# Every third tile of peer_u multiplied whole in fp32 in the first expert pass

## The reference, cut to what matters

```python
    best, pos = lax.top_k(cand, PEER_TOPK)
    eidx = jnp.take_along_axis(cidx, pos, axis=-1)
    gate = jax.nn.softmax(best, axis=-1).astype(h.dtype)
    ...
    def expert_block(args):
        hx, ex, gx = args
        act = jax.nn.gelu(jnp.einsum('td,tkd->tk', hx, u_tab[ex]))
        return jnp.einsum('tk,tkd->td', act * gx, v_tab[ex])
```

## Time and profile before

| | |
|---|---|
| time, median of 3 runs | 3781.97 us (3767.97 to 3790.55) |
| span of the profiled execution | 3785.3 us |
| first expert pass in it | from about 765 to 1495 us |
| second expert pass in it | from 1495 to about 2105 us |
| busy over the span | PE 90%, DVE 70%, PEld 71%, ACT 34%, POOL 12% |

### The profile page before, as it was taken

How to read it: one execution, slowest core, us unless ns; L and a number is a source line. 1 busy time by engine, 2 the same in 40 slices (tenths; PEclk the granted TensorE clock), 3 DMA queues, 4 the chain that set the end, 5 groups by cost and what they waited for, 6 DMA issues and landing times. The chain is left out here.

```text
span 3785.3 us, 43269 instructions
## 1 busy us (share of the span) xinstructions
PE 3422.4 (90%) x17195; PEld 2697.6 (71%) x17195; DVE 2668.2 (70%) x3330; ACT 1280.9 (34%) x1467; POOL 444.0 (12%) x419
## 2 busy tenths in 40 slices
PE   7889878999899999999999799998989898999798
PEld 5755657788899998787877587587845765543676
DVE  6855778889999986778888646665546444894564
ACT  3322333344445544444444333213312011100333
POOL 0011101101121120223322000020001111000000
PEclk8888888999999999999999899999999999999899
DMA  9974367757899998999999453306552112453563
GB/s 356 379 251 126 120 244 288 252 203 291 317 321 354 366 368 305 389 373 372 380 382 379 167 181 107 94 7 219 189 194 84 40 40 78 137 155 115 200 228 145
DMA packets 294600, 870.09 MB, mean 230 GB/s; under 512 B 33584, under 2 KB 108436, under 8 KB 242432
## 3 DMA queue, kind: packets, MB, share of 16 engines
q1 hardware_dynamic: 257616, 670.64, 50.4%
q0 software_dynamic: 34320, 190.40, 13.4%
q10 hardware_dynamic: 2464, 6.29, 0.5%
HBM read 820.22 MB, written 46.38 MB: 229 GB/s over the span
## 5 line engine op out<-in xcount | busy, mean ns | idle before, releaser
L2479 DVE TENSOR_TENSOR expert_w_low<-expert_w,expert_w_high 128x2048 fp32r<-128x2048 f32 x256 | 585.3, 2287 | 149.2 <-ACT expert_w_high L2906 147.1
L2814 PE MATMUL bank<-h_halves,expert_w_high 128*128 128x384 f32 x2048 | 617.2, 372 | 57.3 <-DVE expert_w_low L2479 57.1
L2906 ACT ACTIVATE expert_w_high<-expert_w 128x2048 fp32r<-128x2048 f32 x256 | 490.3, 1915 | 441.8 <-DMA expert_w<-in_peer_v_dram 286.8
L294 DVE TENSOR_TENSOR weights_low<-weights,weights_high 128x1024 fp32r<-128x1024 f32 (+4 forms) x288 | 338.2, 1177 | 296.5 <-ACT weights_high L277 293.1
L2815 PE MATMUL bank<-h_halves,expert_w_low 128*128 128x192 f32 x2048 | 523.0, 255 | 0.0
L277 ACT ACTIVATE weights_high<-weights 128x1024 fp32r<-128x1024 f32 (+4 forms) x288 | 293.5, 1022 | 466.7 <-PE bank L322 383.9
L2814 PEld LDWEIGHTS bank<-h_halves,expert_w_high 128*128 128x128 f32 x2048 | 396.8, 194 | 67.4 <-DVE expert_w_low L2479 66.8
L2815 PEld LDWEIGHTS bank<-h_halves,expert_w_low 128*128 128x128 f32 x2048 | 403.3, 197 | 0.0
L2883 PE MATMUL bank<-expert_w_high,gated_acts_halves 128*128 128x512 f32 x512 | 203.6, 398 | 18.7 <-DVE expert_w_low L2479 18.4
L2885 PE MATMUL bank<-expert_w_high,gated_acts_halves 128*128 128x512 f32 x512 | 203.1, 397 | 0.0
L2884 PE MATMUL bank<-expert_w_low,gated_acts_halves 128*128 128x512 f32 x512 | 202.6, 396 | 0.0
(11 more groups left out here) (721 smaller groups left out, 6840.5 us busy)
## 6 DMA issues: line engine op xcount, KB each, us to landing
expert_w<-in_peer_u_dram SPq DMA_DIRECT2D x128, 1024.0 KB, 6.9
expert_w<-in_peer_v_dram SPq DMA_DIRECT2D x128, 1024.0 KB, 9.5
weights<-in_ada_w_dram SPq DMA_DIRECT2D x88, 512.0 KB, 9.1
weights<-in_w_out_dram SPq DMA_DIRECT2D x32, 1024.0 KB, 13.3
weights<-in_w_in_dram SPq DMA_DIRECT2D x32, 960.0 KB, 8.9
weights<-in_w_in_dram SPq DMA_DIRECT2D x32, 928.0 KB, 9.7
weights<-in_w_in_dram SPq DMA_DIRECT2D x56, 512.0 KB, 7.0
s_gates_w<-in_w_in_dram SPq DMA_DIRECT2D x56, 512.0 KB, 3.7
```

The source lines that it names most:

```text
L294: dve.tensor_tensor(self.low[:, u % self.UNITS_HELD, :, 0:n], self.buf[b][:, k:k + self.UNIT, 0:n], self.high[:, u % self.UNITS_HELD, :, 0 ...
L2479: dve.tensor_tensor(wl[:, n % RING, :], w_sb[:, n % RING, :], wh[:, n % RING, :], ALU.subtract).then_inc(wl_ready, 1)
L2814: pe.matmul(o[:, 0:2 * DENSE], uh[:, b, k, :], acts.both[:, k, :, 0:DENSE], start=(k == 0), stop=False)
L2906: act.activation(wh[:, n % RING, :], w_sb[:, n % RING, :], ACT.Copy).then_inc(wh_ready, 1)
```

## The change

In the first pass the tiles with n % 3 == 2 (`WHOLE_SLOT`, 42 of 128) are no longer split. PE multiplies `w_sb` itself, as fp32, with whole columns of the dense tokens (16 multiplications of 192 columns). These columns are made once (`whole_columns`, two additions on DVE after `own_columns_twice`) and lie in slot 2 of `wh` and `wl`, which the first pass then doesn't use. DVE's `add_halves` becomes a copy for these tiles, ACT makes neither the high half nor the copy of scores. SP may load into slot 2 only after PE has drained the tile before (`whole_used`). The counts of the waits follow (`splits`, `wholes`), and the due times of the DVE order are new: a tile is 5.3 us, of which a dot takes 2.4 and a split 2.7 (a whole tile 0.4); choosing gets the rest, and what it overruns is carried to the next tile.

```diff
@@ -2390,17 +2390,37 @@
     GROUPS, PER_BLOCK = DENSE // TOK, TB // TOK
-    TILE_TIME, TILE_TIME_BESIDE_DOTS = 2.8, 1.9
+    TILE_TIME, DOT_TIME, SPLIT_TIME = 5.3, 2.4, 2.7
+    WHOLE_SLOT = 2
     LISTED = HK * OWN // P
     i1T, i2T, gateT = cols
+    def split(n):
+        return n >= TILES or n % RING != WHOLE_SLOT
+    def splits(n):
+        return sum(split(i) for i in range(n + 1))
+    def wholes(n):
+        return n + 1 - splits(n)
     with ExitStack() as ctx:
         w_sb = m.sb(ctx, "expert_w", [P, RING, D])
-        wh, wl = (m.sb(ctx, f"expert_w_{s}", [P, RING, D], F32R) for s in ("high", "low"))
+        w_at = [(nc.sbuf_base + 31) // 32 * 32]
+        wh = m.sb(ctx, "expert_w_high", [P, RING, D], F32R)
+        w_at.append((nc.sbuf_base + 31) // 32 * 32)
+        wl = m.sb(ctx, "expert_w_low", [P, RING, D], F32R)
         uh, ul = (w[:, :, :].rearrange("p b (k e) -> p b k e", e=P) for w in (wh, wl))
+        w_whole = w_sb[:, :, :].rearrange("p b (k e) -> p b k e", e=P)
+        ON_HIGH = D // DENSE
+        h_whole = [nc.alloc_sbuf_tensor_at(f"whole_columns{i}", [P, n, DENSE], F32, offset=at + WHOLE_SLOT * D * 4)
+                   for i, (n, at) in enumerate(zip((ON_HIGH, KD - ON_HIGH), w_at))]
+        whole_ready, whole_used = m.sem("whole_columns_ready"), m.sem("expert_whole_used")
         act_area = m.sb(ctx, "expert_act", [P, D])
@@ -2475,7 +2495,9 @@
                 def low(n):
-                    dve.wait_ge(wh_ready, n + 1)
+                    if not split(n):
+                        return
+                    dve.wait_ge(wh_ready, splits(n))
                     dve.tensor_tensor(wl[:, n % RING, :], w_sb[:, n % RING, :], wh[:, n % RING, :],
@@ -2504,6 +2526,12 @@
                     dve.tensor_tensor(own_cols.rearrange("p k (s t) -> p k s t", s=2), h, l, ALU.add).then_inc(own_doubled, 1)
+                def whole_columns():
+                    for part, ks in zip(h_whole, (slice(0, ON_HIGH), slice(ON_HIGH, KD))):
+                        h, l = (acts.both[:, ks, i, 0:DENSE].bitcast(F32) for i in range(2))
+                        ins = dve.tensor_tensor(part[:, :, :], h, l, ALU.add)
+                    ins.then_inc(whole_ready, 1)
@@ -2540,8 +2568,11 @@
                     bank = score_ring.get(dve)
-                    dve.wait_ge(half_copied, n + 1)
-                    score_ring.free(dve.tensor_tensor(act_sb[:, g % 2, t, :], bank[:, 0:DENSE], half_scores[:, n % 2, :], ALU.add))
+                    if not split(n):
+                        score_ring.free(dve.tensor_copy(act_sb[:, g % 2, t, :], bank[:, 0:DENSE]))
+                        return
+                    dve.wait_ge(half_copied, splits(n))
+                    score_ring.free(dve.tensor_tensor(act_sb[:, g % 2, t, :], bank[:, 0:DENSE], half_scores[:, splits(n) % 2, :], ALU.add))
@@ -2654,8 +2685,11 @@
                 own_columns_twice()
+                whole_columns()
+                ahead = 0.0
                 for n in range(TILES):
                     plan.tile = n
+                    before = len(plan.dots)
                     if n >= 2:
@@ -2669,13 +2703,14 @@
                     if plan.gates is None:
+                        time = ahead + TILE_TIME - DOT_TIME * (len(plan.dots) - before) - (SPLIT_TIME if split(n) else 0.4)
                         spent = 0.0
-                        time = TILE_TIME if plan.listed is None else TILE_TIME_BESIDE_DOTS
                         while spent < time:
                             spent += us or TILE_TIME
+                        ahead = time - spent
                         continue
@@ -2744,8 +2779,10 @@
                 for n in range(2 * TILES):
-                    if n >= RING:
-                        sp.wait_ge(wl_ready, n - RING + 1)
+                    if n >= RING and split(n - RING):
+                        sp.wait_ge(wl_ready, splits(n - RING))
+                    elif n >= RING:
+                        sp.wait_ge(whole_used, wholes(n - RING))
                     w = io["peer_u"][0] if n < TILES else io["peer_v"][0]
@@ -2808,7 +2845,17 @@
                     b = n % RING
-                    pe.wait_ge(wl_ready, n + 1)
+                    if not split(n):
+                        pe.wait_ge(w_loaded[b], 16 * (n // RING + 1))
+                        pe.wait_ge(whole_ready, 1)
+                        o = score_ring.take(pe)
+                        for k in range(KD):
+                            part, at = divmod(k, ON_HIGH)
+                            mm = pe.matmul(o[:, 0:DENSE], w_whole[:, b, k, :], h_whole[part][:, at, :], start=(k == 0), stop=(k == KD - 1))
+                        score_ring.put(mm)
+                        pe.drain().then_inc(whole_used, 1)
+                        return
+                    pe.wait_ge(wl_ready, splits(n))
                     o = score_ring.take(pe)
@@ -2870,7 +2917,7 @@
                         pe.wait_ge(al_ready, g + 1)
-                    pe.wait_ge(wl_ready, TILES + n + 1)
+                    pe.wait_ge(wl_ready, splits(TILES + n))
                     first, last = n == 0, n == TILES - 1
@@ -2920,10 +2969,12 @@
                     act.wait_ge(score_ring.filled, n + 1)
-                    if n >= 2:
-                        act.wait_ge(score_ring.emptied, n - 1)
-                    act.activation(half_scores[:, n % 2, :], score_ring.banks[n % 4][:, DENSE:2 * DENSE], ACT.Copy)\
-                        .then_inc(half_copied, 1)
+                    if split(n):
+                        freed = [i for i in range(n) if split(i)][-2:-1]
+                        if freed:
+                            act.wait_ge(score_ring.emptied, freed[0] + 1)
+                        act.activation(half_scores[:, splits(n) % 2, :], score_ring.banks[n % 4][:, DENSE:2 * DENSE], ACT.Copy)\
+                            .then_inc(half_copied, 1)
                     high(n + RING)
                         gelu(g - 1)
```

## The result

| | before | changed |
|---|---|---|
| median, first chip (4 runs each) | 3775.82 us (3767.97 to 3790.55) | 3808.06 us (3800.89 to 3817.88) |
| ratio | | 1.0078 (95%: 1.0059 to 1.0098) |
| second chip (30 and 7 runs) | 3778.33 us | 3801.21 us, ratio 1.0065 (1.0042 to 1.0089) |
| span of the profiled execution | 3785.3 us | 3799.1 us |
| first pass, tile 0 to the first tile of the second | 726.8 us | 750.1 us |

The change makes the kernel slower, by 0.65 to 0.78%, 25 to 29 us. The pass itself is 23.3 us longer, so the comparison goes by the pass and its stretches, cut at the same tiles as the earlier trace rows.

What follows compares the result with a forecast made beforehand. DVE was taken to bound most of the first pass, with PE becoming the bound. From 805.2 us, stretches of 78.3, 197, 286 and 119 end at 1485.5 instead of 1495.4: about -10 us, 3772 us, range 3758 to 3790.

Steps and rivals of the forecast that it cites:

- B: First-pass tiles 4 to 19, choosing picks only; forecast at PE's new floor, 78.3 us against 81.7 before.
- C: First-pass tiles 20 to 57, choosing and own-row dot products; forecast 197 us, PE floor 187, before 214.1.
- E: First-pass tiles 58 to 105, one-hot gates and dots; forecast 286 us, PE floor 279, before 279.3.
- F: First-pass tiles 106 to 127, set by transfers and queue order; forecast 119 us, before 118.0.
- Prices: Costs assumed: 0.162 us per fp32 record, 5.61 us per whole tile with 0.42 us drain, `whole_columns` 3.4 us on DVE.
- DVE's relief: Over 42 whole tiles DVE loses a subtraction each, 93 us in all; busy time falls by about 90 us.
- PE as the new bound: First pass: DVE gives up 93 us, PE takes 44 more, so gain ends at PE's new floor.
- some late bursts: Tiles 58 to 105: loads leaving together after PE's drain sometimes land late; 286 us taken over a floor of 279.
- Rival 2: Late bursts idle PE, then half clock: 3.7 us in 14 of 29 three-tile cycles, tiles 20 to 105; 3805 us, chance 0.21.
- Rival 1: PE runs the first pass without gaps, its stretches at their floors: -29 us, 3753 us; chance 0.20.
- Rival 3: Whole tiles cost PE the split price, 4.57 us, with a free drain: -43 us, 3739 us; chance 0.04.
- By volume: Tiles 20 to 105: bytes unchanged, transfers need 178 and 263 us at 377 GB/s, within 6% of PE, not binding.

## Why the prediction was wrong

It gave 3772 us, 10 less than before; the median is 3808.06, and the kernel is 25 to 29 us slower than before: the sign is wrong. Step by step, the changed profile against the forecast:

| | start to tile 4 | B | C | E | F |
|---|---|---|---|---|---|
| before | 33.6 | 81.7 | 214.1 | 279.3 | 118.0 |
| forecast | 36.4 | 78.3 | 197 | 286 | 119 |
| measured | 37.2 | 79.4 | 202.4 | 305.1 | 125.9 |

The pass is 33 us longer than the forecast's; E holds 19 of them, F 7 and C 5.

- **Prices: right.** fp32 records at 0.163 us (0.162 forecast), a whole tile 5.65 (5.61), `whole_columns` 3.42 us on DVE (3.4). The two parts of a whole tile were off in opposite directions: 5.09 us without the drain where 5.19 was taken, and 0.56 for the drain instead of 0.42. That the sum fits so well is luck in part.
- **DVE's relief: right.** Busy 674.5 us before, in the window 765 to 1500; 579.7 over the changed pass.
- **PE as the new bound: right in B only.** The forecast's floors stand (E with the stores cut took 280.9 against 279.3), but nothing from C on ran on them.
- **C, 197 against 202.4.** At one place DVE stands idle for 7 us: SP's score store at 883.4 stands behind a wait for PE, and DVE, which needs the buffer, waits for it:

```profile
894.44 0.36 DVE L2572 COPY expert_act<-bank 128x192 f32<-128x192 f32 x1 [6.91 <-DMA expert_acts<-expert_act]
```

  The forecast named that stores queue behind SP's new wait, and priced nothing for it. At 914.6 DVE waits another 5.7 us for a dot's rows; the whole tiles are not its only cause, as the run with the new due times alone has it too (3.6 us).
- **E, 286 against 305.1: the step that failed.** The term is the +7 us on E's floor for "some late bursts"; measured are +25.8. "Most cycles are just in time and some are late" took the landing times of the earlier trace rows as a spread from which a burst draws, 7.7 us at the median and 15.9 at worst. They aren't one: in the kernel before, every landing of 10 us or more from tile 62 to 112 is one of the three loads behind a gate store. And they did not stay: the forecast had the load of n+4 land after 11 to 15 us, while behind a store and another load it landed after 17 to 18, and the worst load after 20.4. The question was whether each load's lead covers that and 4 us of halves. Before, DVE's pace gave load 75 a lead of 21.0 us; the changed order would have given load 78 one of 16.7, as the load leaves later and PE comes to it earlier. The forecast priced the DVE relief as a gain and did not ask what DVE's lateness had hidden. The cut stores show the cause, with E back at 280.9; how the loss divides between longer landings and shorter leads was not taken apart.
- **F, 119 against 125.9**: the sixth gate store (1394.4) is followed by 10.1 us at tile 110, 4.4 over a whole tile. With the stores cut that stall goes, but F only falls to 122.6; others open up, and why F stays above the forecast is open.
- **Rival 2** had the place, the late burst, and its total of 3805 is within the runs of 3800.9 to 3817.9, in part by luck. Its form was off: not some 14 late cycles of 3.7 us but five in E, of 1.4 to 7.6 us each, with the store and not the burst alone as the trigger, and the gap on PE's gate group rather than on a split tile. Of the half clock it had 1.7 us each; measured 1.2 in three tiles. The Trainium skill (TensorE: Matmul & The Clock Gate, HAM oscillation) warns of waits that keep setting the clock back; this trace agrees in kind and hardly in size: a mean granted clock of 0.97 in E against 0.98 before.
- **Rival 1** (PE gapless) is refuted by E and F and nearly realised in E with the stores cut (280.9 against 279). **Rival 3** falls with the record spacing and 5.65 us a whole tile.
- **By volume** the transfers did not bind, as the forecast had it: cutting five stores of 2 MB, 10 MB of E's 100, gave back 24 us while the DMA share went from 0.86 to 0.84.

What stays open: why a 1 MB load behind a 2 MB store takes up to 18 us. At the 372 GB/s of the earlier trace rows, 2 MB and two loads of 1 MB are 11 us, an estimate; the stores of scores and the indirect row loads that run beside them may take the rest. No run had SP issue the store behind the loads of its burst.

## What to carry to other kernels

When an engine is taken off the critical path, list what its lateness was covering: for each load, compare the time from issue to use with the longest landing, and ask which transfer stands ahead of it and which leave with it. In this kernel the wait moved to a later event in an in-order queue cost next to nothing in E with small stores (280.9 us against 279.3); its price was paid where a large store fell into the burst behind it. Such a change should be judged by stage and kept only where it gains (here before the gate stores begin).

## What the runs showed of the hardware

An fp32 multiplication of 192 columns is two records of 0.163 us each, so a 128x128 by 192 product costs 0.33 us, against 0.285 for the two fp32r multiplications of 384 and 192 columns. A drain of PE in a running stream costs 0.56 us from start to start (5.65 against 5.09 for the tile), more than the one in the earlier trace rows. A 1 MB load issued 0.4 to 0.8 us behind a 2 MB store landed after 16.9 to 18.3 us where the store had left 0.4 to 3.6 us behind another load (changed kernel, second chip), after 10.2 to 13.5 where it had left 5.3 to 8.2 us behind one (due times alone), and in one case of that kind after 15.9 (tile 75 of the kernel before). With a store of 128 KB it was usable after 9.0.
